# Two experts' rows kept on chip, and the sums of the last stage moved from VectorE to TensorE

## The reference, cut to what matters

```
h2 = rms_norm(x)
top_vals, top_idx = top_k(h2 @ w_router + b_router, 4);  gates = softmax(top_vals)
for each expert e and its rows:  gu = rows @ w_gu[e] + b_gu[e]
    act = min(glu, 7) * sigmoid(1.702 * min(glu, 7)) * (clip(lin, -7, 7) + 1)
    y = act @ w_down[e] + b_down[e]
x = x + sum over a token's 4 experts of gate * y
return rms_norm(x, norm_final_w)
```

## Time and profile before

| | us |
|---|---|
| device time, median of 3 | 1245.93 (1244.9 to 1246.02) |
| the profiled execution, its own time | 1245.12 |
| its span | 1243.2 |
| VectorE busy in the span | 1106.8 (89%) |
| TensorE busy, matmuls | 1147.7 (92%) |
| ScalarE busy | 938.6 (75%) |

### The profile page before, as it was taken

How to read it: one execution, slowest core, us unless ns; L and a number is a source line. 1 busy time by engine, 2 the same in 40 slices (tenths; PEclk the granted TensorE clock), 3 DMA queues, 4 the chain that set the end, 5 groups by cost and what they waited for, 6 DMA issues and landing times.

```text
span 1243.2 us, 39998 instructions
## 1 busy us (share of the span) xinstructions
PE 1147.7 (92%) x17556; PEld 887.0 (71%) x17557; DVE 1106.8 (89%) x806; ACT 938.6 (75%) x823; POOL 122.6 (10%) x70
## 2 busy tenths in 40 slices
PE   5999999899999999999999999999999999999984
PEld 3445556888788878877777777777777887777741
DVE  5855677989999999999999999999999999999977
ACT  4434444878888888888888888888888888888861
POOL 0110310027400000000000000000000000000000
PEclk9999999999999999999999999999999999999998
DMA  9606854989999999999999999999999999999976
GB/s 349 229 1 237 271 201 154 347 320 422 419 421 420 419 419 419 418 418 420 416 420 410 417 409 420 408 420 412 418 406 421 409 409 417 410 420 411 419 311 252
DMA packets 73256, 458.08 MB, mean 368 GB/s; under 512 B 10077, under 2 KB 10589, under 8 KB 23633
## 3 DMA queue, kind: packets, MB, share of 16 engines
q1 hardware_dynamic: 68480, 445.30, 88.6%
q0 software_dynamic: 3472, 8.21, 1.7%
q10 hardware_dynamic: 1152, 2.19, 0.5%
HBM read 443.26 MB, written 24.77 MB: 376 GB/s over the span
## 4 chain that ended last, share of the span: by engine, by line
DMA 33%; PE 30%; DVE 17%; issue 11%; ACT 8%; ACTq 0%; DVEq 0%; SPq 0%; POOLq 0%
DMA ring<-in_w_gu_dram 15%; DMA arena<-in_w_gu_dram 14%; DVE ring L417 11%; PE ps L438 9%; PE ps L1132 8%; PE ps L475 5%; ACT ring L414 4%; PE ps L1235 3%; DVE arena L513 2%; PE ps L431 2%; ACT arena L487 1%; DMA ring<-in_w_down_dram 1%; ACT arena L506 1%; DVE arena L480 1%; DMA ring<-in_w_in_dram 1%
## 5 line engine op out<-in xcount | busy, mean ns | idle before, releaser
L417 DVE SCALAR_TENSOR_TENSOR ring<-ring 128x2048 f16<-128x2048 f32 x290 | 654.5, 2288 | 29.3 <-ACT ring L414 28.0
L414 ACT ACTIVATE ring<-ring 128x2048 f16<-128x2048 f32 x290 | 549.9, 1910 | 99.4 <-DMA ring<-in_w_gu_dram 49.8
L438 PE MATMUL ps<-arena,ring 128*128 128x88 f16 x12288 | 506.7, 205 | 40.4 <-issue 26.7
L438 PEld LDWEIGHTS ps<-arena,ring 128*128 128x128 f16 x12288 | 489.8, 100 | 50.8 <-issue 38.5
L475 PE MATMUL ps<-ring,arena 128*88 128x512 f16 x1536 | 337.7, 379 | 4.6 <-DVE arena L519 2.6
L475 PEld LDWEIGHTS ps<-ring,arena 128*88 128x88 f16 x1536 | 181.6, 120 | 147.2 <-issue 4.4
L417 DVE SCALAR_TENSOR_TENSOR ring<-arena,ring 128x2048 f16<-128x2048 f32 x94 | 213.6, 2288 | 20.8 <-ACT ring L414 19.3
L414 ACT ACTIVATE ring<-arena 128x2048 f16<-128x2048 f32 x94 | 179.1, 1908 | 25.6 <-DMA arena<-in_w_down_dram 17.0
L497 POOL DMA_INDIRECT planes<-arena,slot_row x31 | 94.8, 3058 | 943.5 <-ACT arena L522 914.8
L431 PE MATMUL ps<-arena 128*128 128x88 f16 x2048 | 92.7, 205 | 10.1 <-issue 9.8
L431 PEld LDWEIGHTS ps<-arena 128*128 128x128 f16 x2048 | 84.6, 100 | 12.5 <-issue 12.3
(11 more groups left out here) (160 smaller groups left out, 536.9 us busy)
## 6 DMA issues: line engine op xcount, KB each, us to landing
ring<-in_w_gu_dram SPq DMA_DIRECT2D x194, 1024.0 KB, 15.4
ring<-in_w_down_dram SPq DMA_DIRECT2D x96, 1024.0 KB, 15.2
arena<-in_w_gu_dram SPq DMA_DIRECT2D x62, 1024.0 KB, 15.4
arena<-in_w_down_dram SPq DMA_DIRECT2D x32, 1024.0 KB, 16.5
ring<-in_w_in_dram SPq DMA_DIRECT2D x4, 2048.0 KB, 12.5
ring<-planes SPq DMA_DIRECT2D x6, 1024.0 KB, 10.1
ring<-in_w_out_dram SPq DMA_DIRECT2D x2, 2048.0 KB, 8.6
arena<-in_x_dram SPq DMA_DIRECT2D x4, 512.0 KB, 11.7
```

The source lines that it names most:

```text
L414: return act.activation(split_of(slot)[:, 0, :], raw(r), ACT.Copy, scale=SCALE_W)
L417: return dve.scalar_tensor_tensor(split_of(slot)[:, 1, :], raw(r), SCALE_W, split_of(slot)[:, 0, :], ALU.mult, ALU.subtract)
L438: mm = pe.matmul(o, w[:, i, cols], src[:, j, k, :], start=start and n == 0, stop=stop and n == 2, skip_group_check=True)
```

## The change

- The rows of expert E-2 are no longer scaled and scattered. They are copied to `y_kept`, and a second matrix `wg_kept` of its gates is made in `last_gates`, transposed into bank 1 and copied to `wgT_kept`. SP waits for 30 scatters in place of 31.
- `last_gates` moves on VectorE from stage 1 to the start of stage 30, and has two more steps.
- Expert E-1 gets an activation buffer of its own (`actT_last`) and banks 6 and 7 for its rows (`ROWS_LAST`). TensorE no longer waits for the rows of E-2 to leave banks 4 and 5, and ScalarE makes E-1's high activation part before it copies E-2's rows.
- The end is divided anew. For each tile TensorE adds in PSUM: E-2's rows, E-1's rows with the biases, the sum `total`, and the tile's last two planes. VectorE adds only the tile's first two planes to `total`.
- ScalarE squares, and VectorE scales, out of PSUM.
- VectorE's order becomes: sums of tiles 0 and 1, finish 0, sums 2, finish 1, sums 3, finish 2, finish 3.

```diff
 # SP, end
-                sp.wait_ge(scattered, 16 * (E - 1))
+                sp.wait_ge(scattered, 16 * (E - 2))
 # ScalarE, last stage
             glu(E - 1, nth(E - 1, GU_CH))
             high(E // 2, 0, 0)
-            finish_rows(E - 2, nth(E, 0))
-            act_high_part(E - 1)
+            act_high_part(E - 1, actT_last)
             high(E // 2, 0, 1)
+            act.wait_ge(wg_turned, 2)
+            act.activation(wgT, ps[:, 0, :], ACT.Copy).then_inc(wgT_ready, 1)
+            act.activation(wgT_kept, ps[:, 1, :], ACT.Copy).then_inc(wgT_ready, 1)
             high(E // 2, 0, 2)
             high(E // 2, 0, 3)
-            act.wait_ge(wg_turned, 1)
-            act.activation(wgT, ps[:, 0, :], ACT.Copy).then_inc(wgT_ready, 1)
+            act.wait_ge(chunk_used, nth(E, 0))
+            for half in range(2):
+                act_row(act, half, y_kept, 1.0 / (SCALE_A * SCALE_W)).then_inc(row_ready, 1)
             act.wait_ge(pad_cleared, 2)
             act.wait_ge(chunk_used, CH * E)
             for half in range(2):
-                act_row(act, half, y_last, 1.0 / (SCALE_A * SCALE_W)).then_inc(row_ready, 1)
+                act_row(act, half, y_last, 1.0 / (SCALE_A * SCALE_W), ROWS_LAST).then_inc(row_ready, 1)
 # ScalarE, rest
-                    act.wait_ge(acc_ready, 2 * t + 2)
-                    act.activation(pair(2 * t)[:, 0, :], total[:, t, :], ACT.Square, accum_out=ss[:, 12 + t, 0:1])
+                    act.wait_ge(acc_ready, t + 1)
+                    act.activation(pair(2 * t)[:, 0, :].rearrange("p (b c) -> p b c", b=2), ps[:, 2 * t:2 * t + 2, :], ACT.Square, accum_out=ss[:, 12 + t, 0:1])
 # TensorE, last stage
             mm.then_inc(wg_turned, 1)
+            for t in range(NT):
+                mm = pe.transpose(ps[0:CAP, 1, t * P:(t + 1) * P], wg_kept[:, t, :], ident)
+            mm.then_inc(wg_turned, 1)
             most = most_slots(pe)
-            pe.wait_ge(row_ready, 2 * E - 2)
             pe.wait_ge(act_ready, E)
             for j in range(DN_CH):
-                down(E, j, j)
+                pe.wait_ge(low_ready, nth(E, j) + 1)
+                for f in (2 * j, 2 * j + 1):
+                    mm = pe_down(pe, phase(j), f, actT_last, ROWS_LAST)
+                mm.then_inc(chunk_used, 1)
 # TensorE, rest
+                def add(t, w, rows, start=False, stop=False):
+                    for half in range(2):
+                        mm = pe.matmul(ps[:, 2 * t + half, :], w, rows[:, half * 512:(half + 1) * 512],
+                                       start=start, stop=stop)
+                    return mm
+
+                pe.wait_ge(wgT_ready, 2)
+                pe.wait_ge(tail_loaded, 32)
+                pe.wait_ge(row_ready, 2 * E - 2)
+                for t in (0, 1):
+                    add(t, wgT_kept[0:CAP, t * P:(t + 1) * P], y_kept[0:CAP], start=True)
+                pe.wait_ge(row_ready, 2 * E)
+                for t in (2, 3):
+                    add(t, wgT_kept[0:CAP, t * P:(t + 1) * P], y_kept[0:CAP], start=True)
                 for t in range(NT):
+                    add(t, wgT[:, t * P:(t + 1) * P], y_last)
+                for t in range(NT):
+                    pe.wait_ge(sum_ready, t + 1)
+                    add(t, ident, total[:, t, :])
                     pe.wait_ge(pair_loaded[2 * t + 1], 16)
...
+                    for k in range(2):
+                        mm = add(t, ident, pair(2 * t + 1)[:, k, :], stop=k == 1)
+                    mm.then_inc(acc_ready, 1)
 # VectorE, last_gates: two more steps, and its call moves from stage 1 to ahead of stage 30
+                step(dve.tensor_tensor(wg_kept, ranks[:, 0:CAP].unsqueeze(1).to_broadcast([P, NT, CAP]),
+                                       rank1[:, E - 2, :].unsqueeze(2).to_broadcast([P, NT, CAP]), ALU.is_equal))
+                step(dve.tensor_tensor(wg_kept, wg_kept, gdense[:, :, E - 2].unsqueeze(2).to_broadcast([P, NT, CAP]), ALU.mult))
 # VectorE, rest
                     step(dve.tensor_tensor(total[:, t, :], total[:, t, :], pair(2 * t)[:, 0, :], ALU.add))
-                    step(dve.tensor_tensor(total[:, t, :], total[:, t, :], pair(2 * t)[:, 1, :], ALU.add))
-                    dve.wait_ge(pair_loaded[2 * t + 1], 16)
-                    step(dve.tensor_tensor(total[:, t, :], total[:, t, :], pair(2 * t + 1)[:, 0, :], ALU.add))
+                    dve.tensor_tensor(total[:, t, :], total[:, t, :], pair(2 * t)[:, 1, :], ALU.add).then_inc(sum_ready, 1)
...
-                for t in range(NT):
-                    add_planes(t)
-                    add_last(t)
-                    if t >= 1:
-                        finish(t - 1)
-                finish(NT - 1)
+                add_planes(0)
+                add_planes(1)
+                finish(0)
+                add_planes(2)
+                finish(1)
+                add_planes(3)
+                finish(2)
+                finish(3)
```

More of the change, by code:

```diff
@@ L144, in build_program @@
         gdense = wg[:, :, BD:P]
-        wgT = reg_d[:, 512:512 + S]
+        wgT = reg_p[:, 2304:2304 + S]
+        wgT_kept = reg_p[:, 2816:2816 + S]
+        y_kept = reg_p[:, 0:1024]
+        wg_kept = reg_p[:, 0:NT * CAP].rearrange("p (t c) -> p t c", t=NT)
+        actT_last = xT[:, 0]
         fin_w = reg_r[:, 0:1024]
@@ L468, in pe_gu, with pe_down @@
             return mm
-        def pe_down(pe, slot, f):
+        def pe_down(pe, slot, f, acts=actT, rows=ROWS):
             w = split_of(slot)
@@ L474, in pe_down @@
                 for n, (i, j) in enumerate(((0, 0), (0, 1), (1, 0))):
-                    mm = pe.matmul(ROWS[:, half, :], actT[:, j, f, :], w[:, i, col:col + 512], start=f == 0 and n == 0,
+                    mm = pe.matmul(rows[:, half, :], acts[:, j, f, :], w[:, i, col:col + 512], start=f == 0 and n == 0,
                                    stop=f == KD - 1 and n == 2, skip_group_check=True)
@@ L513, in dve_prod, with act_ah, dve_al, act_row @@
             return dve.scalar_tensor_tensor(gub[:, 1], gub[:, 0], SILU_MAX, gub[:, 1], ALU.min, ALU.mult)
[L515 to L522, removed]
+        def act_ah(act, acts=actT):
+            return act.activation(act_parts(0, acts), gub[:, 1], ACT.Copy, scale=ACT_SCALE)
+        def dve_al(dve, acts=actT):
+            return dve.scalar_tensor_tensor(act_parts(1, acts), gub[:, 1], ACT_SCALE, act_parts(0, acts), ALU.mult, ALU.subtract)
+        def act_row(act, half, rows, scale, out_of=ROWS):
+            return act.activation(rows[0:CAP, half * 512:(half + 1) * 512], out_of[:, half, :], ACT.Copy, scale=scale)
         def most_slots(eng):
@@ L739, in add_rows @@
                 pool_scatter(pool, slot_row[0:SCAT, e:e + 1]).then_inc(scattered, 16)
-            for e in range(E - 1):
+            for e in range(E - 2):
                 add_rows(e)
@@ L1094, in rest @@
                 for t in range(NT):
-                    act.wait_ge(acc_ready, 2 * t + 2)
-                    act.activation(pair(2 * t)[:, 0, :], total[:, t, :], ACT.Square, accum_out=ss[:, 12 + t, 0:1])\
+                    act.wait_ge(acc_ready, t + 1)
+                    act.activation(pair(2 * t)[:, 0, :].rearrange("p (b c) -> p b c", b=2), ps[:, 2 * t:2 * t + 2, :], ACT.Square, accum_out=ss[:, 12 + t, 0:1])\
                         .then_inc(ss_ready, 1)
@@ L1419, in rest @@
             def rest():
-                pe.wait_ge(wgT_ready, 1)
+                def add(t, w, rows, start=False, stop=False):
[3 more added lines that the diff above has]
+                    return mm
+                pe.wait_ge(wgT_ready, 2)
+                pe.wait_ge(tail_loaded, 32)
[5 more added lines that the diff above has]
+                    add(t, wgT_kept[0:CAP, t * P:(t + 1) * P], y_kept[0:CAP], start=True)
                 for t in range(NT):
+                    add(t, wgT[:, t * P:(t + 1) * P], y_last)
+                for t in range(NT):
+                    pe.wait_ge(sum_ready, t + 1)
+                    add(t, ident, total[:, t, :])
                     pe.wait_ge(pair_loaded[2 * t + 1], 16)
[L1423 to L1432, removed]
+                    for k in range(2):
+                        mm = add(t, ident, pair(2 * t + 1)[:, k, :], stop=k == 1)
+                    mm.then_inc(acc_ready, 1)
             ending(pe, most, rest, one, skip, last_added)
@@ L1795, in _ @@
                 stage(h, 1)
+            last_gates()
             stage(E // 2 - 1, 0)
```

37 lines of the change are left out of this document (16 added, 21 removed).

## The result

The changed kernel takes 1251.8 us (median of 5, 1250.64 to 1252.94), the kernel before, measured beside it, 1244.9 (1244.38 to 1246.02). The ratio is 1.0050, with a 95% interval of 1.0039 to 1.0062: 6.9 us slower, where 7.1 were forecast. The end is 42.5 us long (1206.25 to 1248.8), and was 33.4 (1209.79 to 1243.2). So it begins 3.5 us sooner and is 9.1 us longer.

A forecast was written before the change was run, and what follows sets the result against it. Weights bound the stages, VectorE the last 50 us; after the change TensorE's adds, from 1207.8, with stall, finish and store end at 1250.3, +7.1 on the span. Forecast 1253.0 us, range 1248.5 to 1258.

The forecast's parts named there:

- The bound and the pace: At the end, TensorE's twenty float32 adds set the time: 0.86 us a matmul, 1.72 an add, 34.4 us in all.
- When the adds start: After the last down product, over near 1207.6, TensorE begins the adds at 1207.8; the last split ends at 1204.2.
- The stall: Before tile 2's adds, TensorE stands 1.1 us waiting for VectorE's sum of that tile, which follows finish 0.
- The last finish and the store: Behind TensorE's last add: 3.7 us to the end of the tile's finish, then 3.4 us for the store.
- The scatter and the loads: Before the final adds: E-2's scatter leaves the path, plane loads are wholly hidden, in by some 1223.5; no plane wait.
- The branch: Between last down product and first add: a branch taken while the array still works, 0 at least, 1.9 us at most.
- The gates: VectorE's gate steps moved from stage 1 to stage 30: no gain (bound 1.65 us) and no cost (1.7 without cover).
- The sum: Whole kernel: 1245.12 + 7.1 = 1252.2, with 0.8 to the median 1253.0 us.
- A fallen clock: During TensorE's adds: the clock falls to 1.2 GHz, giving 1258 us for ten microseconds of it, 1287 for all; 5%.
- The planes: Rival at the last weight loads: planes queued behind them make the last chunks up to 5 us late, 1257 us; 5%.
- The cheap adds: Rival on TensorE's final adds: float32 entries overlap when dense, 0.43 us a matmul, 1240.7 us, faster by 5.2; 5%.
- the change is worth nothing on the path: Rival: gates' move gains 1.65 us, no stall, downs a microsecond sooner, 1248 to 1249 us; 5%.

The follow-up runs named there:

- e2: Changed kernel with only VectorE's order altered: sums of tiles 0, 1, 2, finish 0, sums 3, then finishes 1 to 3; 1250.6 us, 1.0041 of the kernel before.
- e4: Changed kernel with TensorE adding each tile's total twice, 24 adds in place of 20; 1257.2 us, 1.0102 of the kernel before.
- e3: Changed kernel with TensorE at 14 adds, VectorE adding four planes of tiles 0, 1 and three of 2, 3, all sums before finishes; 1240.8 us, again 1240.5.
- e5: Changed kernel with the end divided as in the kernel before, E-2's rows still kept on chip; 1243.3 us, 0.9985 of the kernel before.
- e9: Changed kernel with GpSimd adding each tile's second plane pair, TensorE making 13 adds tile by tile; 1244.2 us, 0.9993 of the kernel before.
- e6: Changed kernel with the gates' five steps moved back to stage 1; 1251.8 us, 1.0052 of the kernel before.
- e1: Changed kernel with all four planes of each tile back on VectorE, TensorE making 12 adds, all rows first; 1251.2 us, 1.0046 of the kernel before.
- e7: Against e1, TensorE's same 12 adds ordered tile by tile in place of all rows first; 1241.4 us, 0.9967 of the kernel before.

## Why the prediction was right

**The bound and the pace.** The step that everything rested on was 0.86 us for a float32 matmul, read from the chain's 1.73 us for four entries and carried to a run of eighty. It held: 0.43 us an entry in the changed kernel, 34.35 us for eighty in e2. The timeline's burst of eight, which the prediction shows for the same pace, is 3.70 us long and alone would give 0.46 an entry, 2.6 us more for eighty; the rows of the chain were the right ones to take. e4 shows the slope apart from all else.

By the two sentences of the Trainium skill that the prediction names (Perfetto Trace Analysis, Engine Utilization; TensorE: Matmul & The Clock Gate, Back-to-back issue gap) the estimate was half of that pace, and the kernel would have been faster by 5 us. The measurement decides: nothing in any trace here shows a whole float32 matmul of 512 columns in 0.43 us.

**When the adds start.** Predicted 1207.8, in this profile 1206.25. The steps inside are as worked out: the activation's high part no longer waits for E-2's copy, the four down products follow one another with hardly a wait (48 entries in 10.84 us). But the whole stream was 1 to 1.5 us sooner in this execution: the high part began at 1192.31 and not at 1193.65, and the last split ended at 1203.0 and not at 1204.2, which the prediction had named as a sign of being wrong. The nine other profiles of kernels with the same stages and the same gates have the last down product over between 1205.8 and 1210.2, the middle one at 1207.3. A step of 1.5 us of one profile's start is within that scatter, and the forecast of 1207.6 for that product lies near its middle. The branch cost nothing: the adds begin at 1206.09 in TensorE's timeline.

**The stall.** Predicted 1.1 us of TensorE for tile 2's sum, shown 0.94; in e2 it is gone, and the end is 1.2 us shorter.

**The last finish and the store.** Predicted 3.7 and 3.4; from 1241.81 on the chain has 3.63 to 1245.44, and the span ends 3.4 later. The scaling out of PSUM takes 1.28 us, as out of SBUF; the square 1.02, even 0.04 less.

**The scatter and the loads.** They are off the path, as said. One sentence was wrong: that there would be no wait for a plane. VectorE waits 3.23 and 2.61 us for the first planes of tiles 0 and 1. It costs nothing, since TensorE asks for the first of those sums at 1219.8. In e3 and e5, where VectorE's chain is tight, the landings do set its first sums; e9's rows below show them, two pairs in 5 us.

**The gates.** Taken as nothing, both ways; e6 agrees, within its interval of 1.7 us.

**The sum.** The span's change was predicted as +7.1 and is +5.6 in this profile, the difference being the start of the adds; the medians, in which that scatter is averaged, have +6.9 and, the second time, +7.0. That the forecast came within 0.2 us owes something to luck: the interval of the measurement is 1.4 us to either side. The lower end of the forecast's own range is off by 1 us: the terms named for it (1.65, 1.1 and a few tenths) lead from 1253.0 to about 1250 and not to 1249. Nothing hangs on it.

**The rivals.** A fallen clock did not occur in the changed kernel (1.00 through the adds), but e1 shows that it was a fair one: the same adds, with a VectorE that keeps TensorE waiting, do fall to 0.50. The planes did not get in the way of the last weights: these took 15.2 to 16.0 us from issue to landing, the last one before 16.6. The cheap adds are refuted. That the change is worth nothing on the path, 1248 to 1249 us, is refuted too: all of the adds are on the path, and the gates' move shows no gain in e6.

## What to carry to other kernels

Before work is moved from a busy engine to an idle one, price it there, at that engine's pace for that data type: a float32 sum of a 128x1024 tile was 1.24 us on VectorE and 1.72 on TensorE, so halving VectorE's sums, from 16 to 8, for twelve adds more on TensorE changed the bound and did not remove it. With 14 adds on TensorE the kernel gained 5 us, with 20 it lost 7. A change of several parts wants each part timed by itself: here one was worth 2 us and was buried under another's 8.5. And the order of the instructions on the new bound counts as much as their number: 12 adds in one order and in another were 9 to 10 us apart.

## What the hardware showed that I had not expected

**An idle TensorE is paid for at the next product.** In e1 four float32 entries took 3.78 us after idle pieces of 6.89 and 3.29 us, with a granted clock of 0.59 and then 0.50; in e7, after pieces of 1.6 us, 1.98, at 1.00. e9 has it too, and there it lies on the path:

```profile
1227.71 5.40 PE L1439 MATMUL ps<-arena,sm 128*128 128x512 f32 x8 [4.48 <-DVE arena L1883]
...
1232.94 1.88 PE L1439 MATMUL ps<-ring,sm 128*128 128x512 f32 x4
...
1227.70:1229.60 1.90, 1.89 (x3) 0.86 (x4) 1.87 (x2) 0.00 (x0) 0.00 (x0) 0.52 0.00 0
```

After 4.48 us of idleness the clock is 0.52, and twelve entries take 7.1 us where 5.2 are their pace: 2 us.

**GpSimd and VectorE wait for one another.** GpSimd's sums of 128x1024 in e9:

```profile
1208.15 2.35 POOL L772 TENSOR_TENSOR ring<-ring 128x1024 f32<-128x1024 f32 x1 [21.69 <-DMA ring<-planes]
1213.27 3.15 POOL L772 TENSOR_TENSOR ring<-ring 128x1024 f32<-128x1024 f32 x1 [2.78 <-DMA ring<-planes]
1218.30 2.35 POOL L772 TENSOR_TENSOR arena<-arena 128x1024 f32<-128x1024 f32 x1 [1.88 <-DMA arena<-planes]
1223.30 3.28 POOL L772 TENSOR_TENSOR ring<-ring 128x1024 f32<-128x1024 f32 x1 [2.65 <-DMA ring<-planes]
```

and VectorE's timeline beside them:

```profile
1212.99 1.22 DVE L1879 TENSOR_TENSOR arena<-arena,ring 128x1024 f32<-128x1024 f32 x1
...
1218.44 2.23 DVE L1489 SCALAR_TENSOR_TENSOR rstd<-nwt,rstd 128x1 f32<-128x1 f32 x1
...
1223.15 1.22 DVE L1879 TENSOR_TENSOR arena<-arena 128x1024 f32<-128x1024 f32 x1
...
1224.41 3.25 DVE L1883 TENSOR_TENSOR arena<-arena 128x1024 f32<-128x1024 f32 x1
```

The small step of one column (L1489) that takes 0.16 us elsewhere took 2.23, and ended at 1220.67, where GpSimd's sum ended at 1220.65. The GpSimd sums that began while a VectorE sum was under way, at 1213.27 and 1223.30, took 3.15 and 3.28: the rest of that VectorE sum (to 1214.21 and 1224.37) and then 2.2, near the 2.35 of the first one, which met no VectorE instruction. VectorE's next sum then waited for GpSimd in its turn, 3.25 for 1.22. TensorE stood 4.48 us for that sum of tile 2. So in these rows they do not slow each other in part; one stands until the other's instruction is over. On the chain that ended last this costs 0.8 us (3.15 for 2.35), 2.1 (2.23 for 0.16) and 2.0 (3.25 for 1.22); with the 2 us of the clock it is 6.9, enough for the 6.4 by which the end missed its forecast.

The Trainium skill says this: SBUF — State Buffer, section SBUF: two separate sides, has the port pair that the two share as an exclusive lock for the whole instruction, taken by a GpSimd operation or, against a GpSimd operation that reads SBUF, by a VectorE operation with two SBUF inputs. The rows agree with it: 3.15 and 3.28 us on the one side, 2.23 and 3.25 on the other. I had it only as the rival, and had not put a price on it. That it is this lock and no other cause was not tried by itself.
